# A second place for three quarters of a sample's gathered blocks, loads reordered by time, and a step of the sample's softmax moved by one unit and to another engine

## The reference, cut to what matters

```
top_v, top_i = lax.top_k(imp, n_sel)
gather = jax.vmap(jax.vmap(lambda a, i: a[i]))
k_sel = gather(ks_g, top_i).reshape(b, C_KV_HEADS, t, n_sel * CMP_BLOCK, HEAD_DIM)
v_sel = gather(vs_g, top_i).reshape(b, C_KV_HEADS, t, n_sel * CMP_BLOCK, HEAD_DIM)
s_s = jnp.einsum('btgrd,bgtmd->bgrtm', q, k_sel, ...) * scale
p_s = masked_softmax(s_s, sel_ok)
o_s = jnp.einsum('bgrtm,bgtmd->btgrd', p_s, v_sel)
...
return gates[..., 0:1] * o_c + gates[..., 1:2] * o_s + gates[..., 2:3] * o_w
```

## Time and profile before

| | us |
|---|---|
| median of 3 runs | 2132.23 |
| the profiled execution, its own time | 2134.37 |
| its span in the trace | 2132.4 |
| attention, first L958 to the first L371 of the output projection | 1433.55 to 1931.67 |
| PE busy in the span | 1966.2 |
| DVE busy | 791.4 |
| ACT busy | 573.9 |
| POOL busy | 696.0 |

### The profile page before, as it was taken

The page is one execution under the profiler, slowest core; times in us unless marked ns, Lnnn a source line. Parts: engine busy times, 40 slices in busy tenths (PEclk is TensorE's granted clock), DMA queues, the critical chain, the costliest instruction groups (busy, mean ns, idle before and its releaser), DMA issues.

```text
span 2132.4 us, 41056 instructions
## 1 busy us (share of the span) xinstructions
PE 1966.2 (92%) x15800; PEld 1819.2 (85%) x15800; DVE 791.4 (37%) x1151; ACT 573.9 (27%) x925; POOL 696.0 (33%) x790
## 2 busy tenths in 40 slices
PE   6999999999999999999999999998676877769999
PEld 6999999999999999999999999985444544438999
DVE  4343433436433533333233333325333433434221
ACT  6212111122222321112122223224333443333211
POOL 3444445445300155465355520011233222220000
PEclk9999999999999999999999999999898998889999
DMA  9798988999854666866632343543343233333543
GB/s 290 166 208 190 195 190 181 204 197 202 193 148 130 185 202 179 237 187 172 154 80 79 76 111 105 133 132 107 110 129 101 88 117 107 109 97 101 147 120 84
DMA packets 357249, 316.69 MB, mean 149 GB/s; under 512 B 17866, under 2 KB 316035, under 8 KB 356323
## 3 DMA queue, kind: packets, MB, share of 16 engines
q1 hardware_dynamic: 308034, 192.39, 32.3%
q0 software_dynamic: 36000, 112.80, 24.0%
q10 hardware_dynamic: 13072, 9.57, 1.5%
HBM read 291.14 MB, written 40.76 MB: 156 GB/s over the span
## 4 chain that ended last, share of the span: by engine, by line
PE 66%; DMA 14%; SPq 6%; DVE 4%; issue 4%; POOL 4%; ACT 2%; ACTq 0%; DVEq 0%; POOLq 0%
PE main L371 54%; DMA block_sum<-cache_cmp_kv,block_row 11%; SPq L432 3%; SPq L429 2%; PE aux L958 2%; PE main L993 2%; PE main L979 1%; POOL v_norm L2154 1%; POOL block_sum L2127 1%; DVE a_max L1903 1%; PE aux L809 1%; PE main L1003 1%; PE main L1047 1%; DVE probs L1912 1%; PE aux L1106 1%
## 5 line engine op out<-in xcount | busy, mean ns | idle before, releaser
L371 PE MATMUL main<-act_hi,w_hi 128*128 128x260 f32 x4128 | 842.6, 285 | 11.8 <-DVE act_lo L632 3.2
L371 PE MATMUL main<-act_hi,w_lo 128*128 128x260 f32 x4128 | 834.0, 284 | 0.0
L371 PE MATMUL main<-act_lo,w_hi 128*128 128x260 f32 x4128 | 832.8, 283 | 0.0
L371 PEld LDWEIGHTS main<-act_hi,w_hi 128*128 128x128 f32 x4128 | 638.9, 189 | 15.2 <-issue 10.9
L371 PEld LDWEIGHTS main<-act_hi,w_lo 128*128 128x128 f32 x4128 | 638.7, 189 | 0.0
L371 PEld LDWEIGHTS main<-act_lo,w_hi 128*128 128x128 f32 x4128 | 638.3, 189 | 0.0
L359 DVE TENSOR_TENSOR w_lo<-w_raw,w_hi 128x2048 fp32r<-128x2048 f32 x129 | 295.2, 2288 | 142.7 <-ACT w_hi L354 131.9
L2127 POOL DMA_INDIRECT block_sum<-cache_cmp_kv,block_row x128 | 233.5, 1824 | 256.3 <-DMA block_sum<-cache_cmp_kv,block_row 243.3
L354 ACT CAST w_hi<-w_raw 128x2048 fp32r<-128x2048 f32 x129 | 245.6, 1904 | 233.1 <-PE main L371 207.1
L432 POOL DMA_DIRECT2D sel_kv<-cache_sel_kv x208 | 124.6, 599 | 486.0 <-issue 301.9
L1903 DVE TENSOR_REDUCE a_max<-aux 128x1 f32<-128x128 f32 (+3 forms) x128 | 62.5, 488 | 258.1 <-PE aux L960 258.0
(11 more groups left out here) (280 smaller groups left out, 1475.4 us busy)
## 6 DMA issues: line engine op xcount, KB each, us to landing
w_raw<-w_in_odd SPq DMA_DIRECT2D x56, 1024.0 KB, 5.7
w_raw<-w_in_even SPq DMA_DIRECT2D x39, 1024.0 KB, 6.2
w_raw<-w_out_even SPq DMA_DIRECT2D x16, 1024.0 KB, 7.3
w_raw<-w_out_odd SPq DMA_DIRECT2D x16, 1024.0 KB, 6.9
win_kv_sample_out<-state_win_kv SPq DMA_DIRECT2D x8, 2044.0 KB, 11.4
sel_kv<-cache_sel_kv POOLq DMA_DIRECT2D x208, 64.0 KB, 2.3
sel_kv<-cache_sel_kv SPq DMA_DIRECT2D x208, 64.0 KB, 2.5
win_k<-win_kv_sample_out SPq DMA_DIRECT2D x8, 1024.0 KB, 6.0
```

The lines of the kernel that those rows point to most:

```text
L371: ins = nc.tensor.matmul(MP[:, slot, b, 0:HALF], w_[:, slot, k, :], x_[:, k, b * HALF:(b + 1) * HALF], start=(k == 0 and q == 0), stop=(k ...
```

## The change

1. Three of the four parts get a second place: `SKV[b][a]`, b = s % 2, for a = 0, 1, 2, in halves of the places of `w_raw`, `w_hi` and `w_lo` that were used before or lay idle. Part 3 of both sets is one and the same place. Each place has semaphores of its own (`landed`).
2. SP and POOL issue in another order: at the turn of a sample first part 3 of this sample, then, in the course of the sample, parts 0 to 2 of the next one. These wait for `pv_done` of sample s-1 of the same place. The gates and the window's keys are put between them. The first weight tile of the output projection, which SP loaded ahead of the attention into one of the places, is now loaded in the last sample. POOL loads the prompt's first values after parts 0 to 2 of the first sample and no longer between them.
3. `PROB_STEP` is 15: PE turns the blocks' probabilities a unit later, the copies to `SPT` are ACT's (`selected_out`), and they stand ahead of that unit's exponential. `sample_scores` of the window, `window_max`, `window_exp`, `sample_weights`, the value products, `sample_out`, `sample_rows` and `sample_store` each move on by one unit.
4. Seven semaphores of the compressed branch are merged into two (`c4_pe`, `c4_dve`), with the same order of waits.

Nothing is computed otherwise, and the number of transfers and instructions on PE stays.

```diff
+        for b_ in range(2):
+            SKV.append([at(f"sel_kv{b_}{a_}", off + (8 * 1024 if a_ < 3 and not b_ else 0), [P, 2, 2, 512])[0]
+                        for a_, off in enumerate((RAW_OFF, WHL_OFF, WHL_OFF + 16 * 1024, SKA_OFF))])
...
+        def free_pairs(queue, s, a):
+
+            if a == 3:
+                if s:
+                    queue.wait_ge(sem("pv_done"), 4 * s)
+            elif s >= 2:
+                queue.wait_ge(sem("pv_done"), 4 * s - 7 + a)
+            elif a == 0:
+                queue.wait_ge(w_split, N_ODD_OUT + 1 + s)
+            else:
+                queue.wait_ge(mm_done, N_ODD_OUT + 1 + s)
...
-        PROB_STEP = 14
+        PROB_STEP = 15
...
-            load_w(sp, N_ODD_OUT, (N_ODD_OUT // 2, N_ODD_OUT % 2), w_oout[:, :, 0:P])
...
+            for a in range(3):
+                key_blocks(0, a)
+            sp.wait_ge(sem("z_out"), 16 * HEADS + 16)
+            gate_load(0)
             for s in range(NS):
...
+                key_blocks(s, 3)
+                forced_load(nc.sync, s, PAGES - 1, 64, SKV[s % 2][3][0:64, 1], landed("ks", s, 3))
...
                 if s < NS - 1:
+                    key_blocks(s + 1, 0)
+                    gate_load(2 * s + 1)
                     sp.wait_ge(sem("k_turned"), 12 * s + 4)
                     window_half(nc.sync, s + 1, KWK, 0, sem("kwk_landed"))
+                    key_blocks(s + 1, 1)
+                    key_blocks(s + 1, 2)
+                    gate_load(2 * s + 2)
+                else:
+                    gate_load(2 * s + 1)
+                    sp.wait_ge(sem("pv_done"), 4 * s - 3)
+                    load_w(sp, N_ODD_OUT, (N_ODD_OUT // 2, N_ODD_OUT % 2), w_oout[:, :, 0:P])
...
                 if w % 16 == PROB_STEP:
                     pe.wait_ge(sem("p_evac"), 3 * s + 1)
-                elif w % 16 == PROB_STEP + 1:
-                    pe.wait_ge(sem("p_evac"), 3 * s + 3)
+                elif w % 16 == 0 and s:
+                    pe.wait_ge(sem("p_evac"), 3 * s)
...
-                if u == 6 and w < UNITS:
+                if u == 7 and w < UNITS:
                     sample_scores(s, 0)
...
-                if u == 15:
-                    window_values(s)
-                    selected_values(s, 0)
-                    selected_values(s, 1)
                 if u == 0 and s:
+                    window_values(s - 1)
+                    selected_values(s - 1, 0)
+                    selected_values(s - 1, 1)
+                if u == 1 and s:
                     selected_values(s - 1, 2)
                     selected_values(s - 1, 3)
-                if u == 2 and s:
+                if u == 3 and s:
                     sample_out(s - 1)
...
+            def selected_out(w, s):
+
+                act.wait_ge(sem("p_turned"), 2 * s + 1)
+                if s:
+                    act.wait_ge(sem("pv_done"), 4 * s)
+                nc.scalar.copy(SPT[:, 0:4].rearrange("p t n -> p (t n)"), MP[:, 0, w % 2, :]).then_inc(
+                    sem("p_evac"), 1)
...
                     keys_out(w, s, KEY_STEP[u])
+                if u == PROB_STEP:
+                    selected_out(w, s)
                 if w + 2 < UNITS:
                     exp4(w + 2)
                 probs_out(w)
...
-                    if u == 13:
+                    if u == 14:
                         sample_weights(s)
...
+            for a in range(3):
+                key_blocks(0, a)
+            pool.wait_ge(mm_done, N_ODD_OUT + 2)
+            prompt_values(0)
             for s in range(NS):
+                key_blocks(s, 3)
...
+                if s < NS - 1:
+                    for a in range(3):
+                        key_blocks(s + 1, a)
```

More of the change, by code:

```diff
@@ L554, in gate_load @@
                 nc.sync.dma_start(SZH[:, h % 2], szT_scr[h]).then_inc(sem(f"sz_landed{h % 2}"), 16)
-            def free_pairs(queue, s, a):
-                if s:
-                    queue.wait_ge(sem("pv_done"), 4 * s - 3 + a)
-                elif a == 1:
-                    queue.wait_ge(w_split, N_ODD_OUT + 2)
-                elif a == 2:
-                    queue.wait_ge(mm_done, N_ODD_OUT + 2)
-            for s in range(NS):
-                if s == 0:
-                    sp.wait_ge(sem("chain_pe"), 4)
-                    window_half(nc.sync, 0, KWK, 0, sem("kwk_landed"))
-                else:
-                    gate_load(2 * s)
-                for a in range(4):
-                    free_pairs(sp, s, a)
-                    for r in range(4 * a, min(4 * a + 4, NSEL_FREE)):
-                        for g in range(2):
-                            block_load(nc.sync, s, g, r, sem(f"ks_landed{a}"))
-                    if a == 0 and s:
-                        gate_load(2 * s + 1)
-                    if a == 2 and s == 0:
-                        sp.wait_ge(sem("z_out"), 16 * HEADS + 16)
-                        gate_load(0)
-                        gate_load(1)
-                forced_load(nc.sync, s, PAGES - 1, 64, SKV[3][0:64, 1], sem("ks_landed3"))
-                nc.sync.dma_start(SKV[3][64:65, 1], O["sel_kv_sample"][s:s + 1].rearrange("a (k c) -> a k c", k=2)
-                                  ).then_inc(sem("ks_landed3"), 16)
@@ new lines, in key_blocks @@
+            def key_blocks(s, a):
+                free_pairs(sp, s, a)
+                for r in range(4 * a, min(4 * a + 4, NSEL_FREE)):
+                    for g in range(2):
+                        block_load(nc.sync, s, g, r, landed("ks", s, a))
+            sp.wait_ge(sem("chain_pe"), 4)
+            window_half(nc.sync, 0, KWK, 0, sem("kwk_landed"))
+            for a in range(3):
+                key_blocks(0, a)
+            sp.wait_ge(sem("z_out"), 16 * HEADS + 16)
+            gate_load(0)
@@ L599, in odd_loads @@
                     if first and c == 1:
-                        sp.wait_ge(sem("pv_done"), 4 * NS - 2)
+                        sp.wait_ge(sem("pv_done"), 4 * NS - 3)
                     if not (first and c == 0):
@@ L1044, in turn_keys @@
                         else:
-                            tile, n = page_pair(t_)
+                            tile, n = block_pair(s, t_ - 4)
                             src = tile[0:n, 0, g * P:(g + 1) * P]
@@ L1103, in selected_values @@
                 for p in (2 * q, 2 * q + 1):
-                    tile, n = page_pair(p + 4)
+                    tile, n = block_pair(s, p)
                     for g in range(KV):
@@ L1422, in keys_out @@
                         sem("k_evac"), 1)
+            def selected_out(w, s):
[4 more added lines that the diff above has]
+                    sem("p_evac"), 1)
+                act.wait_ge(sem("p_turned"), 2 * s + 2)
+                nc.scalar.copy(SPT[:, 4:7].rearrange("p t n -> p (t n)"),
+                               MP[:, 0, (w + 1) % 2, 0:3 * P]).then_inc(sem("p_evac"), 1)
+                nc.scalar.copy(SPT[0:NEWROW, 7], MP[0:NEWROW, 0, (w + 1) % 2, 3 * P:4 * P]).then_inc(
+                    sem("p_evac"), 1)
             def window_exp(s):
@@ L1446, in _ @@
                 probs_out(w)
-                if u == 7:
+                if u == 8:
                     window_exp(s)
```

85 lines of the change are left out of this document (34 added, 51 removed).

## The result

| | before | after |
|---|---|---|
| median of 4 runs each on one chip, us | 2130.47 (2128.67 to 2133.68) | 1989.95 (1988.80 to 1990.33) |
| ratio, 95% interval | | 0.9336 [0.9316, 0.9356] |
| span of the profiled execution, us | 2132.4 | 1988.0 |

The change takes 140.5 us off, 6.6%. The forecast was 2004 with a range of 1990 to 2032.

The account below looks back on a forecast made before the run. PE, busy 92%, was held to lose time in the attention, mostly waiting for chosen blocks' keys, with slow restarts. Terms 113 + 13 + 3 - 1 = 128 us take 2134.4 to 2006, as a median 2004; range 1990 to 2032.

Parts of the forecast that it names:

- The first term: Attention, PE's waits for chosen blocks' keys: seven periods fall from 437 to 323 us, gain taken as 113.
- the move of the window's steps: Attention, window's scores and exponential from units 6 and 7 to 7 and 8: cost 0, bounds 2 either way.
- The second term: Attention, blocks' probabilities turned a unit later with copies on ACT: gain 13 us, bounds 22 and -11.
- the two ends: End of the attention: gain 3 us, between 0 and 5; its start: loss 1, between 0 and 3.
- The 0.4 for the second slot: At the turn of probabilities: about 0.4 us more until ACT has copied unit 14's probabilities and freed the slot.
- The 0.3 for unit 17's exponential behind the copies: After the turn: ACT's exponential of unit 17 and copy of unit 15 stand behind the three copies, 0.3 us.
- The loss of 1 for the prompt's later values: Start of the attention: POOL issues the prompt's first values behind parts 1 and 2; loss 1 us, between 0 and 3.
- The signs: Profile after: key turns' DMA waits under 5 us, periods 43 to 46, clock 1.00, turn and copy waits 1.3 a sample.
- ACT as the new wait: Rival: ACT's copies hold back unit 17's exponential, the turn's gain is lost; 2028 us, chance 0.10.
- SP's queue as the bound: Rival: slow issues make a sample's loads on SP take 49 us, 4.5 more than PE needs; 2035 us, chance 0.06.
- Part 3 late: Rival: part 3's single place, or a gate ahead, keeps one wait at u = 11, 7 us; 2053 us, chance 0.05.
- The lower clock: Rival: many short pauses get PE the lower clock in the attention, up to 36 us a sample; 2256 us, chance 0.02.

Follow-up runs that it names:

- loads_only: Kernel after with the later turn, ACT's copies and the window's move undone, keeping second places and new load order; 2015.62 us, ratio 0.9465.
- window_early: Kernel after with the window's scores, maximum and exponential back at units 6, 6 and 7; 1995.64 us, ratio 0.9370.
- places_old_order: Kernel after with its second places, but both queues in the load order of the kernel before; 2110.34 us, ratio 0.9909.
- two_doubled: Kernel after with second places for parts 0 and 1 alone; 1990.44 us, ratio 0.9339.
- one_doubled: Kernel after with a second place for part 0 alone; 2053.15 us, ratio 0.9627.

## Where the prediction was right, and which terms of it were too small

The sum of the prediction beside the profiled executions, us:

| term | predicted | measured | from |
|---|---|---|---|
| blocks' waits, seven periods | 113 | 113.90 | 437.14 - 323.24 (loads_only) |
| turn a unit later, copies on ACT | 13 | 16.25 | 323.24 - 306.99 (window_early) |
| window's steps a unit later | 0 | 5.23 | 306.99 - 301.76 |
| end of the attention | 3 | 4.25 | 16.80 - 12.55 |
| start of the attention to the first turn | -1 | 1.97 | 44.18 - 42.21 |
| outside the attention | 0 | 2.80 | 1.65 ahead of it, 1.15 behind |
| sum | 128 | 144.4 | 2132.4 - 1988.0 |

**The first term** came out, with all it rests on: sample 0 is the model for the others (in loads_only odd periods are 44.8 to 45.1 us and even ones 47.8 to 48.0, forecast at 45.0 and 47.8), the slow restart goes with the wait (PE's busy time in the periods fell by 33 us, none of it from fewer instructions), and the queues keep up. That it came out within 1 us is in part luck, since executions of the kernel before scatter over 5. Had the waits alone been counted, 79.5, it would have been three tenths too small. The prediction did not tell the places and the order apart; by places_old_order the places are worth little without the order.

**The step that failed** is the move of the window's steps, put at nothing ("Cost 0, bounds 2 either way") where it measured 5.2. The second term and the two ends were too small as well, so that nothing cancelled:

- The window's move. The prediction did name the 0.72 us wait of the even samples, three of them 2.2 us. It missed the second wait of the same place, for ACT's copy of keys, which the same move shortens, in odd samples too. By waits, the two kinds are 8.5 + 2.9 = 11.4 us in window_early and 5.4 after; 0.7 of this comes back as waits for DVE's scaling. The cost was put at nothing because the pieces are short; what counts is which operation stands behind them.
- The second term: 13 forecast, 16.25 measured. Of the turn's waits 1.3 us a sample was to be left (the four pieces named, 0.3, 0.4, 0.2 and 0.3, add to 1.2). In the seven ordinary samples (4.7 - 1.34) / 7 = 0.48 is left before the turn, where 0.3 was forecast. The 0.4 for the second slot came as 0.28, within the turn: it takes 1.37 us (L1097, sample 1) and not the 1.09 of the last sample and of the kernel before, and ACT's copy of unit 14, which frees the slot, ends at 1517.00, 0.66 us after the turn's start. Before the product after the copy it is (1.8 - 0.68) / 7 = 0.16, forecast 0.2. The 0.3 for unit 17's exponential behind the copies did not come. In all 0.92 is left, and 3.2 - 0.92 = 2.3 us in seven samples are 16.
- The ends gave 6.2, not 2. Sample 0's turn stands ahead of the seven periods; its wait fell from 1.87 to 0.36 us. The 13 counts seven turns with this one among them, and leaves out the last sample's, 2.50 before and 1.34 after. The loss of 1 for the prompt's later values did not come: no wait for them stands in the trace after. At the tail the term had the wait of 3.33 us but not its slow restart. The sample's first value products, in the trace of before:

```profile
1921.11 1.93 PE L1096 MATMUL aux<-win_v,win_p_t 128*32 128x128 f32 x32
1922.82 1.69 PE L1106 MATMUL aux<-sel_kv,p_t 128*32 128x128 f32 x32
```

After, the same two take 1.08 and 1.06 us (the rows of the end, above).

The profiled executions differ by 144.4 us and the medians by 140.5: that of before took 2134.37, 3.9 above the median of its four runs. The table's last term, 2.8 us, is no part of the change that the traces can name: over the runs the attention began between 1427 and 1434 us, whatever the kernel.

**The signs and the rivals.** The signs came in the main; the periods are 42.2 to 44.2 us where 43 to 46 were named, and 0.9 us a sample is left at the turn, not 1.3. ACT as the new wait: no; its 1.8 us before L1005 and the 0.28 within the turn are all there is of it. (The 10.5 to 14 us that the prediction gives for ACT's busy time are 10.5 to 12.3 in the earlier trace rows; 13.8 and 14.6 are DVE's.) SP's queue as the bound: no; it waits 4.4 us a sample for part 3's place, and it kept up even with two places (two_doubled). Part 3 late: not here, but it is the first thing to go when the places become fewer (one_doubled). The lower clock: no; the seven periods ran at 1.00 with some 50 short waits, the longest 1.34 us. The second failure mode that the Trainium skill describes ("TensorE: Matmul & The Clock Gate", "A second HAM failure mode"), a clock that swings with frequent short idles, did not show in them.

**What stays open.** The contributions are differences of single traces, good to about 1 us where the periods repeat; those of the kernel before run from 60.9 to 63.9 us, so the first is less sure. The merged semaphores and the moved weight tile were not run by themselves; they are in the first term. The three steps of the window were moved together, and what each is worth is read from the trace. That ACT is the better place for the copies rests on 3.4 us in one trace.

## What to carry to other kernels

A second buffer pays only when the loads into it can be issued early: read the issuing engine's queue in order, and look for a transfer in it that waits for something late. Two of the three second places were enough here, and with none at all two moved loads gave 42 us of the 140. The places without the order gave nothing that can be told apart. Count a short step's cost by what stands behind it on its engine, not by its own length: a maximum and an exponential of 0.7 us each, a unit too early, cost PE 1.35 us in an even period.

## What the runs showed of the hardware

A part's last transfers can be late because of a large one in another queue. The last that SP issues for part 3, a block of 256 KB and the new token's row (4 KB), count one semaphore. PE went on 2.9 us after the row's issue where the DMA engines had room (1501.91 to 1504.78, share 0.38), and 7.6 and 8.4 us after it where POOL had issued 1 MB some 2 to 3 us ahead (share 1.01 and 1.00). Holding POOL's load back, with SP's queue as it was, took most of these waits away (42.1 to 10.6 us, and 29.2 to 6.4). The Trainium skill says ("DMA: Bandwidth & Descriptors", "Issuing engines are not separate DMA queues") that transfers of all issuing engines run on the same 16 DMA engines and interleave; the runs agree with the sharing. They do not show what a row of 4 KB alone would have waited, nor how the engines took turns: in sample 1 of one_doubled the 1 MB took 8.6 us to land, and PE went on 2.1 us after that. The wait is booked on the transfer issued last, with no hint of the other queue.
